# Tile-by-tile inputs, stride-4 scores on VectorE and column halves side by side in the samples' mix tile

## The reference

```python
xn = _rmsnorm(x, g_pre)
u = xn @ w_in          # gq gk gv gg | glr | dq dk dv (3 groups x 4 heads x 128) | dg | ga gb
q, k, v = ...          # 4 heads, key 128, value 256
log_a = log_sigmoid(glr @ w_gla_lr + b_gla_lr) / 16
o_a, s_new = _gla(q, k, v, log_a, gla_s0)          # chunks of 64
y_a = (_rmsnorm(o_a, g_gla_norm) * silu(gg)) @ w_gla_branch
for g, (win, dil) in enumerate(((128, 1), (512, 4), (2048, 16))):
    # each query reads the 129 keys at t - dil*m: of the prompt, or of the sample's cache and its new tokens
    o_g, lse_g, nbuf = ...
o_b = weighted_by_softmax(lse, o)
y_b = (o_b * silu(dg)) @ w_dil_branch
merged = sigmoid(ga) * y_a + sigmoid(gb) * y_b
h = x + _rmsnorm(merged @ w_out, g_post)
h = h + (pe @ w_ple_proj) * sigmoid(h @ w_ple_gate)
```

## Time and profile before

| | us |
| --- | --- |
| median of 3 runs | 2875.69 (2873.54 to 2880.13) |
| the profiled execution, its own time | 2874.96 |
| its span in the trace | 2873.2 |
| TensorE (PE) busy | 2824.2 |
| VectorE (DVE) busy | 1077.1 |
| ScalarE (ACT) busy | 873.7 |
| GpSimd (POOL) busy | 375.7 |

### The profile page before, as it was taken

The page is one execution under the profiler, slowest core; times in us unless marked ns, Lnnn a source line. Parts: engine busy times, 40 slices in busy tenths (PEclk is TensorE's granted clock), DMA queues, the critical chain, the costliest instruction groups (busy, mean ns, idle before and its releaser), DMA issues.

```text
span 2873.2 us, 41107 instructions
## 1 busy us (share of the span) xinstructions
PE 2824.2 (98%) x16336; PEld 1490.4 (52%) x16336; DVE 1077.1 (37%) x2416; ACT 873.7 (30%) x1791; POOL 375.7 (13%) x609
## 2 busy tenths in 40 slices
PE   7999999999999999999999989999999999999998
PEld 4444455665545665566555545555544444444444
DVE  4211134444332443344223323343323455555532
ACT  5201023444322322333123321111113444444431
POOL 0000010101222001130011023332200000000000
PEclk9999999999999999999999999999999999999999
DMA  6234444545468565574476769898846965665541
GB/s 210 90 116 134 142 163 158 200 168 196 161 231 285 171 201 183 186 238 159 169 264 221 220 174 328 282 307 279 273 166 197 282 176 161 169 170 148 152 107 33
DMA packets 293992, 550.80 MB, mean 192 GB/s; under 512 B 153453, under 2 KB 158389, under 8 KB 289817
## 3 DMA queue, kind: packets, MB, share of 16 engines
q1 hardware_dynamic: 242746, 289.37, 33.0%
q0 software_dynamic: 51056, 258.81, 27.2%
HBM read 378.05 MB, written 236.67 MB: 214 GB/s over the span
## 4 chain that ended last, share of the span: by engine, by line
PE 93%; DMA 3%; DVE 2%; SPq 1%; issue 1%; ACT 1%; POOL 0%; DVEq 0%; POOLq 0%
PE out L2475 41%; PE out L2082 21%; PE out L2472 14%; PE out L1072 2%; PE out L1057 2%; PE out L2478 2%; PE out L1063 1%; PE out L568 1%; PE out L578 1%; PE out L579 1%; PE out L1352 1%; PE out L1048 1%; PE out L1312 1%; DMA sw_rows<-U 1%; DMA sw_kc<-in_cache_kv_w 1%; PE out L543 1%
## 5 line engine op out<-in xcount | busy, mean ns | idle before, releaser
L2475 PE MATMUL out<-w_hi,xn_hi 128*128 128x512 f16 x1920 | 729.2, 380 | 0.0
L2475 PE MATMUL out<-w_lo,xn_hi 128*128 128x512 f16 x1920 | 728.7, 380 | 0.0
L2475 PE MATMUL out<-w_hi,xn_lo 128*128 128x512 f16 x1920 | 728.6, 379 | 0.0
L2387 ACT ACTIVATE stage<-out 128x512 f32<-128x512 f32 (+1 forms) x170 | 99.4, 585 | 914.9 <-PE out L2475 657.6
L2419 DVE TENSOR_SCALAR stage<-out 128x512 f32<-128x512 f32 (+1 forms) x170 | 114.9, 676 | 627.1 <-PE out L2475 457.1
L2475 PEld LDWEIGHTS out<-w_hi,xn_lo 128*128 128x128 f16 x1920 | 188.1, 98 | 227.2 <-issue 1.1
L2475 PEld LDWEIGHTS out<-w_hi,xn_hi 128*128 128x128 f16 x1920 | 188.7, 98 | 205.3 <-issue 6.8
L2475 PEld LDWEIGHTS out<-w_lo,xn_hi 128*128 128x128 f16 x1920 | 188.2, 98 | 201.3 <-issue 0.8
L2472 PE MATMUL out<-xn_hi,w_hi 128*128 128x512 f16 x640 | 242.8, 379 | 2.2 <-DVE w_lo L2358 2.1
L2472 PE MATMUL out<-xn_hi,w_lo 128*128 128x512 f16 x640 | 242.6, 379 | 0.0
L2472 PE MATMUL out<-xn_lo,w_hi 128*128 128x512 f16 x640 | 242.6, 379 | 0.0
(11 more groups left out here) (307 smaller groups left out, 4056.4 us busy)
## 6 DMA issues: line engine op xcount, KB each, us to landing
out<-in_cache_kv_w POOLq DMA_DIRECT2D x64, 1020.0 KB, 8.8
U<-stage SPq DMA_DIRECT2D x240, 256.0 KB, 5.1
raw<-in_w_in SPq DMA_DIRECT2D x80, 512.0 KB, 5.1
sw_kc<-in_cache_kv_w POOLq DMA_DIRECT2D x24, 1024.0 KB, 13.7
sw_vc<-in_cache_kv_w POOLq DMA_DIRECT2D x24, 1024.0 KB, 9.8
UT<-stage SPq DMA_DIRECT2D x80, 256.0 KB, 3.0
sw_rows<-U POOLq DMA_DIRECT2D x32, 512.0 KB, 9.6
out<-in_cache_kv_w POOLq DMA_DIRECT2D x16, 1008.0 KB, 9.6
```

The costliest lines, as they stand in the source:

```text
L2387: move_out(act, m, lambda o, x: act.activation(o, x, ACT.Copy, scale=1.0 / W_SCALE))
L2475: last = pe.matmul(out[m % 3][:, :], x[:, k, at:at + P], y[:, k, :], start=first, stop=final)
```

## The change

Four parts:

- **Inputs.** `ORDER` starts with `U_GV`, which isn't turned, so that the first slots need one token tile each. `Inputs` works per token tile in a ring of eight x tiles; the gain is loaded as a 128 x 1024 broadcast and multiplied in on VectorE with the norm. The first four tiles are still turned on TensorE (8 transposes each, L307), the other 13 are cut by rows (`split_hi`, `split_lo`) and turned by DMA on SP's queue (`turn_rows`). Two more buffers (`raw_first`) let the first four weight pieces load at once.
- **Samples.** Group 1 joins group 2 in `ROWED`: eight steps a sample, one a slot (`EVERY` = 1, `FIRST` = 1), a ring of four, two flips at slot 9, value products at slot 13. The first values are asked for two slots into sample 0. Six instead of five cache copies are issued per column until all are out.
- **The samples' tile in the mix** (`beside(t)`, t = 16): the two column halves of 512 are made side by side in partitions 0 to 63 and 64 to 127 of one PSUM bank, and the element by element work runs on 128 partitions. The halves' sums of squares are exchanged by two small DMAs (`swap_means`).
- **The passage.** The preparation of tile 2 comes after the last slot's move-out, and the gate's hi weights are loaded with those of out.

The core of the diff:

```diff
-ROWED = (2,)
+ROWED = (1, 2)
-ORDER = ([U_GQ, U_GK, U_GV, U_GV + BANK]
+ORDER = ([U_GV, U_GQ, U_GK, U_GV + BANK]
-SAMPLE_SLOT, SAMPLE_PERIOD = 526, 15
+SAMPLE_SLOT, SAMPLE_PERIOD = 527, 15
 class Inputs:
-    GROUPS = [(BANK // P, P)] * (SEQ // BANK) + [(1, SAMPLES)]
-    TILES = BANK // P
+    RING = 8
+    FIRST = 4
+    UNITS = FIRST * SLOTS
...
+    def scale(self, dve, t):
+        if t == 0:
+            dve.wait_ge(self.g_loaded, 16)
+        dve.wait_ge(self.rstd_ready, t + 1)
+        dve.scalar_tensor_tensor(out=self.tile(t), in0=self.tile(t), scalar=self.rstd[:self.rows(t), t:t + 1], in1=self.g[:self.rows(t), :],
+                                 op0=ALU.mult, op1=ALU.mult).then_inc(self.scaled, 1)
...
+    def turn_rows(self, sp, t):
+        n, rows = t - self.FIRST, self.rows(t)
+        sp.wait_ge(self.row_lo, n + 1)
+        for part, xn in enumerate((self.xn_hi, self.xn_lo)):
+            sp.dma_start_transpose(xn[:, :, t * P:t * P + rows], self.row[n % 2][part][:rows, :]).then_inc(self.row_turned[n % 2], 16)
...
+    def tensor(self, pe, slot):
+        t, half = divmod(slot, SLOTS)
+        if half == 1 and t + 2 < self.FIRST:
+            self.turn(pe, t + 2)
...
 class Samples:
-    EVERY = 2
-    RING = 3
-    FLIP_SLOT = EVERY * (STEPS - 1) + 1
-    FREED_SLOTS = {0: 3, 1: 4, 2: 5, 3: 9, 4: 5}
+    EVERY = 1
+    RING = 4
+    FIRST = 1
+    FLIP_SLOT = FIRST + EVERY * (STEPS - 1) + 1
+    VALUE_SLOT = 13
+    FREED_SLOTS = {0: 3, 1: 6, 2: 8, 3: 10, 4: 3}
...
 class Mix:
-    PREPARE_SLOT = LOAD_SLOT + 12
+    PREPARE_SLOT = LOAD_SLOT + 11
-    THIRD_SLOT = MERGE_SLOT + 4
+    THIRD_SLOT = COLUMN_TILES * TILE_SLOTS - 1
...
+    def half(self, t, banks, n):
+
+        if self.beside(t):
+            part = slice(n * BANK // 2, (n + 1) * BANK // 2)
+            return banks[0][:, part], part
+        return banks[n][:, :], slice(n * BANK, (n + 1) * BANK)
...
+    def swap_means(self, sp):
+
+        t = self.TILES - 1
+        after(sp, self.m_step, t * 3 + 1)
+        for c in range(2):
+            sp.dma_start(self.other_mean[c * SAMPLES:(c + 1) * SAMPLES, :], self.mean_m[(1 - c) * SAMPLES:(2 - c) * SAMPLES, 0:1]) \
+              .then_inc(self.means_swapped.sem, 16)
...
         self.load_weights(sp, "out", self.w_hi, self.cut_hi)
         self.load_weights(sp, "out", self.w_lo, self.cut_lo)
+        self.load_weights(sp, "gate", self.w_hi, self.cut_hi)
...
                 for n in range(2):
-                    made = pe.matmul(out[n][:rows, :], a[:, k, :rows], b[:, at + k, n * BANK:(n + 1) * BANK],
-                                     start=(k == 0 and i == 0), stop=(k == last and i == 2))
+                    w = b[:, at + k, n * BANK:(n + 1) * BANK]
+                    if not self.beside(t):
+                        x, made = a[:, k, :], out[n][:, :]
+                    else:
+                        c, j = divmod(k, BANK // P) if name in ("out", "gate") else (0, k)
+                        x, made = a[:, j, c * SAMPLES:(c + 1) * SAMPLES], out[0][n * SAMPLES:(n + 1) * SAMPLES, :]
+                    made = pe.matmul(made, x, w, start=(k == 0 and i == 0), stop=(k == last and i == 2))
...
-                    for piece in pieces[:2 if at == 6 else 1]:
+                    count = 2 if at < TOKEN_TILES - 1 else 1
+                    for piece in pieces[:count]:
```

More of the change, by code:

```diff
@@ L231, in __init__ @@
         self.lo_ready = one("lo_ready")
+        self.row_hi = one("row_hi")
+        self.row_lo = one("row_lo")
+        self.row_turned = [one(f"row_turned{s}") for s in range(2)]
     def left(self):
[L235 to L251, removed]
+        n = TOKEN_TILES
@@ L259, in start @@
         pool.wait_ge(self.power_ready, 1)
[L261 to L270, removed]
@@ L345, in tensor, with square @@
-    def tensor(self, pe, slot):
-        i, u = self.coming(slot)
-        if i is not None and 3 <= u < 7:
-            for k in (2 * u - 6, 2 * u - 5):
-                self.turn(pe, i, k)
-    def wait_half(self, pe, i, half):
-        pe.wait_ge(self.lo_ready, i * K_TILES + (half + 1) * K_TILES // SLOTS)
+    def square(self, act, t):
+        rows = self.rows(t)
+        act.wait_ge(self.x_loaded[t % self.RING], 16 * (t // self.RING + 1))
+        wait(act, self.squared, t - 1)
+        act.activation(self.squares[t % 2][:rows, :], self.tile(t), ACT.Square, scale=D_MODEL ** -0.5,
+                       accum_out=self.mean[:rows, t:t + 1]).then_inc(self.squared, 1)
@@ new lines, in place, with turn @@
+    def place(self, t, c):
+        n, rows = t * SLOTS + c, self.rows(t)
+        ks = slice(c * K_TILES // SLOTS, (c + 1) * K_TILES // SLOTS)
+        return n, self.bank[n % len(self.bank)][:, :].rearrange("p (k t) -> p k t", t=P)[:, :, :rows], ks, slice(t * P, t * P + rows)
+    def turn(self, pe, t):
+        rows = self.rows(t)
+        pe.wait_ge(self.scaled, t + 1)
+        for c in range(SLOTS):
+            n, bank, ks, _ = self.place(t, c)
+            wait(pe, self.lo_ready, n + 1 - len(self.bank))
+            for j, k in enumerate(range(ks.start, ks.stop)):
+                last = pe.transpose(bank[:, j, :], self.tile(t)[:, k * P:(k + 1) * P], self.identity[:rows, :rows])
+            last.then_inc(self.turned, 1)
@@ L2069, in vector, with product @@
             self.h_lo_half(dve, t - 1)
-    def product(self, pe, out, parts, name, rows):
+    def product(self, pe, out, parts, name, t):
         hi, lo = parts
```

399 lines of the change are left out of this document (233 added, 166 removed).

## The result

| | before | with the change |
| --- | --- | --- |
| median | 2874.61 (4 runs) | 2855.38 (4 runs, 2852.19 to 2856.77) |
| ratio | | 0.9928, 95% interval 0.9911 to 0.9945 |
| TensorE busy | 2824.2 | 2776.1 |
| the profiled execution's span | 2873.2 | 2850.4 |

A forecast was written before the change was run, and what follows sets the result against it. TensorE, busy for 98% of the span, was taken to bound the kernel. Gains of 18 (A), 12 (B) and 20 (C) less 3 (D) make 47, from 2874.96 to 2828 us; range 2809 to 2852.

The forecast's parts named there:

- A: Start: first projection matmul at 14.0 us, column 0 over at 103.7 instead of 122.5; gain 18.
- C: Samples' tile of the mix: column halves side by side take half the matmul time; gain 20 us (14 to 21).
- rival 4: Samples' tile of the mix: the halves don't run side by side at 512 columns; 2848 us, chance 0.05.
- D: Passage to the mix: last move-out goes first, but TensorE waits for out weights; loss 3 us (8 to gain of 2).
- the third load of weights: Passage: gate's hi weights (2 MB) share the queues, delaying the out weights or z(2)'s transposes by up to 4.8 us.
- B: Samples' stage: group 1's scores moved from TensorE to VectorE; 28 - 8.4 - 4.5 - 3, gain 12 us.
- TensorE's work off: Samples' stage: TensorE loses four blocks of work, 3.5 us in each of 8 samples, 28 in all.
- VectorE's lateness: Samples' stage: flips wait for VectorE's eight steps, 12.4 us in sum against 4.0 of waits now; net -8.4.
- the first sample's wait: First sample: new_k lands about 7 us later behind row loads and kc pieces, 2.6 filled by a slot; -4.5.
- the fourth: Samples' row loads: ring of four delays steps 5 to 8 by 1.7 us at 8.9 landing; -3 for all samples.
- Rival 1: Samples' stage: row loads set the pace; landing of 14 us decides, at 19 the kernel takes 2915; chance 0.03.
- The prediction's alarm for this stage: Samples' stage: TensorE's idle time above 30 us would show the forecast wrong in sum.

The follow-up runs named there:

- e3: The changed kernel with the passage part undone (tile 2 prepared where it was, gate's hi weights loaded later): 2851.83 us.
- e11: The changed kernel with flips a slot later, samples three slots later with first loads issued as before, and all of the passage part undone: 2823.07 us.
- e10: The changed kernel with flips a slot later and all samples three slots later, their first loads still issued at slot 522: 2822.1 us.
- e9: The changed kernel with flips a slot later and the gate's hi weights loaded after the transposes of m(1) again: 2829.79 us.
- e5: The changed kernel without the row loads beyond the first four (60 of 64 left out), all VectorE steps kept: 2825.66 us.
- e1: The changed kernel with the samples part undone, group 1's scores on TensorE again: 2841.53 us.
- e4: The changed kernel with the samples, samples' tile and passage parts undone; only the start and the earlier cache copies left: 2859.77 us.
- e8: The changed kernel with all row loads issued on SP's queue instead of GpSimd's: 2877.71 us.
- e13: The changed kernel without the values of samples 1 to 7, the products using sample 0's values: 2855.7 us.
- e7: The changed kernel with the first sample's new keys asked for ahead of its cached keys and rows: 2850.56 us.

## Why the prediction was wrong

**A, the start: right.** 18 forecast, 20.1 in the trace of the change. The pieces hold too (first transpose 9.12, first matmul 13.76, column 0 over at 102.35). What was left out is that a gain ahead of a stage that waits for loads may not arrive whole: alone A is worth 15.4.

**C, the samples' tile: right.** 20 forecast, 19.5 measured; rival 4 is out. GpSimd waited 2.5 for the exchange of the means (2.7 forecast), and the wait before gate(16) is 1.8 instead of 1.5.

**D, the passage: right in kind.** 3 lost forecast. By the medians undoing D gains 3.5 in e3, where the times overlap, and loses 1.0 in e11 against e10; undoing its half in e9 gains 1.1. So a loss isn't shown, and it is at most about what was forecast. The wait did go from the last move-out to the out weights, where the lower clock then came, as said; against what was said, the third load of weights has no part in it, since the wait is as long without it:

```profile
2228.37 1.01 PE L2182 MATMUL out<-mix_w_hi,mix_mTh 128*128 128x512 f16 x2 [7.94 <-DMA mix_w_lo<-CUT_LO]
```

**B, the samples: a gain of 12 forecast, a loss of 14 measured.** Of its four terms three held. Without row loads, so with TensorE's work off, VectorE's lateness and the first sample's wait all in, e5 stands at 2825.66, 15.9 below e1; the sum of these three terms was 28 - 8.4 - 4.5 = 15.1. VectorE's lateness measured 14.4 for 12.4. Here some luck is in it: the lines above that 12.4 give 22.5 - 20.7 = 1.8 in six samples and 22.5 - 18.3 = 4.2 in two, 19 in all, and the 1.2, 2.3 and 3.6 written there come to 13.1; how 12.4 came about isn't said. The first sample's wait grew from 11.9 to 16.2, by 4.3 where 4.5 were forecast. The step that failed is the fourth: "That delays steps 5 to 8 by 1.7, much of it behind VectorE's own lateness; I take -3 for all samples." The runs put 29.7 in its place (e5 against the change), of which the two traces show 19.9 as idle time of TensorE and 6.2 as the same work at a lower clock. The 1.7 itself was too small by a little (landings of 9.9 instead of 8.9), and three things were wrong with the step:

- *The two latenesses add.* A reload waits for the end of a step, so what makes VectorE late makes the load late, and the loads' landing comes on top. I took the larger of the two.
- *The median of before was the wrong row.* It came from loads that went out one in 5 us. With one per step, four are out together, and the ones that the flips waited for landed in 8 to 12 us, in the first sample in 15.5.
- *A stall can cost more than its length.* In the trace of the change each of 3 us or more was followed by a stretch at the lower clock, 1.2 to 1.8 us for 24 matmuls. The prediction had this effect in the passage only.

Rival 1 had the mechanism and put its point of decision at a landing of 14; by the sum above the flip is later from 7.6 on, and with 15.9 / 8 = 2 us a sample to lose, B is worth nothing from 9.6 on, earlier with the clock (an estimate; no run varied L alone). Its chance, 0.03, stood for a kernel slower than before; the same mechanism at the landings seen, taking all of B and no more, was no case of its own. The prediction's alarm for this stage, idle time above 30 us, stayed silent at 20.8; the spacing of the value products, 48.8 instead of 46.3, told it.

## What to carry to other kernels

A ring that refills behind a consumer adds its landing to the consumer's own delay; price it as end of the step that frees the buffer + issue + landing, and compare that with the slot of the one who waits, before work is moved to an engine "with room on average". When work is moved off the bounding engine, look for the first place where that engine waits for the new owner, and give that wait a slot of slack: here one line gave 24.5 us, where the part was forecast at 12. Take a landing from a stretch that is as dense as the changed kernel will be.

## What the hardware showed that was not expected

- A load that writes 512 KB from 4 KB of DRAM, the same for all partitions, lands in 10 us at the median beside other traffic, with 23 MB of it more or less. Leaving such loads out (52 in the stage) took DMA's share of the stage from 0.90 to 0.56 and the landing of the 1 MB loads of keys from 15.5 to 5.7 us; leaving 23 MB of values out took the share to 0.75 and left the keys at 16.2.
- Issued on SP's queue, among its stores and weight pieces, such a load lands in 12.5 us instead of 9.9, and the keys' loads left on the first queue land in 11.6 instead of 15.5.
- What a stall of TensorE does to its clock isn't the same each time. In nine traces (the change, e1, e4 to e8, e10, e13) every stall of 4.1 us or more before a flip was followed by slow matmuls (24 in 6.36 to 7.91 us instead of 5.18; 12 in 4.06 instead of 2.59). After stalls of 2.7 to 4.0 us it went either way: 3.97 was followed by 6.37 in the change and by 5.18 in e10, 3.13 by 6.87 in the change and by 5.18 in e7. After 2.1 us or less all ran at full speed.
